# GpSimd splits each unit of weights in four pieces of 128x256 in place of one instruction over 128x1024

## The reference, cut to what matters

```python
def first_block(x, ...):
    u = rmsnorm(h, norm_mix[i])
    proj = u @ w_in[i]                      # attention and gated delta net inputs
    attn_out = sliding_window_sink_attention(aq, ak, av, sinks[i])
    dn_out = gated_deltanet(dq, dk, dv, dz, db, da, ...)
    h = h + jnp.concatenate([attn_out, dn_out], axis=-1) @ w_o[i]
    m = rmsnorm(h, norm_mlp[i])
    h = h + jnp.square(jax.nn.relu(m @ w_up[i])) @ w_down[i]
    gate = jax.nn.sigmoid(rmsnorm(h, norm_ple[i]) @ w_ple_gate[i])
    h = h + gate * (p[i] @ w_ple_proj[i])
    return rmsnorm(h, norm_final)

def second_block(x, ...):
    u = rms_norm(x, norm_mix_g[l]) @ w_in[l]
    y_pool, y_hgrn = pool_mixer(...), hgrn2_mixer(...)      # gated recurrence, 6 heads of 128
    x = x + jnp.concatenate([y_pool, y_hgrn], axis=-1) @ w_out[l]
    x = x + jnp.square(jax.nn.relu(rms_norm(x, norm_mlp_g[l]) @ w_up[l])) @ w_down[l]
    return rms_norm(x, final_norm_g)
```

## Time and profile before

| what | us |
|---|---|
| median of 3 runs | 2521.81 (2514.71 to 2522.38) |
| the profiled execution, device time | 2521.18 |
| its span in the profile | 2519.4 |
| PE busy | 2390.0 |
| DVE busy | 1881.2 |
| POOL busy | 1071.2 |
| ACT busy | 943.3 |

### The profile page before, as it was taken

How to read it: one execution, slowest core, us unless ns; L and a number is a source line. 1 busy time by engine, 2 the same in 40 slices (tenths; PEclk the granted TensorE clock), 3 DMA queues, 4 the chain that set the end, 5 groups by cost and what they waited for, 6 DMA issues and landing times. The chain is left out here.

```text
span 2519.4 us, 38470 instructions
## 1 busy us (share of the span) xinstructions
PE 2390.0 (95%) x15284; PEld 1899.3 (75%) x15284; DVE 1881.2 (75%) x2356; ACT 943.3 (37%) x1488; POOL 1071.2 (43%) x675
## 2 busy tenths in 40 slices
PE   8887999899999999999999999999999999999997
PEld 6655777687788877888777778777777888778885
DVE  3676666646878889888947677777568877988887
ACT  3154223214433334443514244444253333443433
POOL 3411222233555555454544433343445555555542
PEclk9998999999999999999999999999999999999998
DMA  4200000211244375434112111111314344644332
GB/s 162 68 17 17 27 27 27 80 48 42 103 173 147 138 246 182 157 126 167 42 65 95 53 34 35 35 35 43 117 34 147 138 146 162 244 167 151 131 123 99
DMA packets 109709, 254.99 MB, mean 101 GB/s; under 512 B 9312, under 2 KB 9568, under 8 KB 107360
## 3 DMA queue, kind: packets, MB, share of 16 engines
q1 hardware_dynamic: 104112, 233.82, 27.3%
q10 hardware_dynamic: 5424, 18.75, 2.2%
HBM read 182.28 MB, written 67.63 MB: 99 GB/s over the span
## 5 line engine op out<-in xcount | busy, mean ns | idle before, releaser
L681 PE MATMUL pairs<-x_hi,w_hi 128*128 128x512 f32 x1592 | 545.2, 407 | 36.5 <-DVE x_lo L1755 16.4
L681 PE MATMUL pairs<-x_lo,w_hi 128*128 128x512 f32 x1592 | 530.6, 397 | 0.8 <-issue 0.8
L681 PE MATMUL pairs<-x_hi,w_lo 128*128 128x512 f32 x1592 | 527.7, 396 | 0.8 <-issue 0.8
L681 PEld LDWEIGHTS pairs<-x_hi,w_hi 128*128 128x128 f32 x1592 | 286.9, 190 | 118.8 <-issue 37.8
L645 POOL TENSOR_TENSOR idle<-idle 128x1 f32<-128x1 f32 x78 | 19.5, 250 | 781.7 <-PE pairs L681 772.2
L681 PEld LDWEIGHTS pairs<-x_hi,w_lo 128*128 128x128 f32 x1592 | 299.4, 190 | 64.4 <-issue 0.9
L681 PEld LDWEIGHTS pairs<-x_lo,w_hi 128*128 128x128 f32 x1592 | 298.3, 190 | 62.9 <-issue 1.3
L664 POOL TENSOR_TENSOR w_lo<-w_raw,w_hi 128x512 fp32r<-128x512 f32 x150 | 238.1, 1596 | 230.1 <-ACT w_hi L1278 230.0
L681 PE MATMUL pairs<-work_r,w_hi 128*128 128x512 f32 x1072 | 329.9, 391 | 4.8 <-DVE work_r L1751 2.1
L681 PE MATMUL mid<-work_r,w_hi 128*128 128x512 f32 x992 | 309.6, 393 | 17.8 <-DVE work_r L1751 12.1
L664 POOL TENSOR_TENSOR w_lo<-work,w_hi 128x512 fp32r<-128x512 f32 x128 | 178.0, 1392 | 216.7 <-ACT w_hi L1278 216.7
(11 more groups left out here) (217 smaller groups left out, 3920.9 us busy)
## 6 DMA issues: line engine op xcount, KB each, us to landing
h_ops<-work SPq DMA_DIRECT2D x224, 256.0 KB, 4.4
w_raw<-w_stream SPq DMA_DIRECT2D x81, 512.0 KB, 3.5
w_raw<-w_up SPq DMA_DIRECT2D x120, 256.0 KB, 3.8
out_sq<-h_ops SPq DMA_DIRECT2D x28, 1024.0 KB, 5.2
x_lo_raw<-h_ops SPq DMA_DIRECT2D x28, 1024.0 KB, 5.1
work<-w_down SPq DMA_DIRECT2D x16, 1024.0 KB, 6.8
out_sq<-w_down SPq DMA_DIRECT2D x8, 1024.0 KB, 7.3
x_lo_raw<-w_down SPq DMA_DIRECT2D x8, 1024.0 KB, 5.5
```

Of the source, the lines that this page charges most:

```text
L681: return nc.tensor.matmul(out, w, x, start=start, stop=stop)
```

## The change

`split` issues the copy as four instructions over 256 columns each and the subtraction as four more. The waits and the signals stay: `w_hi_done` is raised by the last piece of the copy, `w_split` by the last piece of the subtraction.

```diff
+            PIECES = [slice(n * QUARTER, (n + 1) * QUARTER) for n in range(4)]
+
             def split(slot, loaded, started, n):
                 pool.wait_ge(w_loaded[slot], loaded)
                 if started is not None:
                     pool.wait_ge(unit_started, started)
                 nc.gpsimd.tensor_tensor(idle[:, 0:1], idle[:, 1:2], idle[:, 1:2], ALU.add)
-                nc.gpsimd.tensor_scalar(w_hi[:, slot, :], w_raw[:, slot, :], 1.0, None, ALU.mult).then_inc(w_hi_done, 1)
+
+                for part in PIECES:
+                    ins = nc.gpsimd.tensor_scalar(w_hi[:, slot, part], w_raw[:, slot, part], 1.0, None, ALU.mult)
+                ins.then_inc(w_hi_done, 1)
                 pool.wait_ge(w_hi_done, n + 1)
-                nc.gpsimd.tensor_tensor(w_lo[:, slot, :], w_raw[:, slot, :], w_hi[:, slot, :],
-                                        ALU.subtract).then_inc(w_split, 1)
+                for part in PIECES:
+                    ins = nc.gpsimd.tensor_tensor(w_lo[:, slot, part], w_raw[:, slot, part], w_hi[:, slot, part], ALU.subtract)
+                ins.then_inc(w_split, 1)
```

## The result

| | before | after |
|---|---|---|
| median | 2519.72 (2514.71 to 2522.38, 4 runs) | 2489.32 (2485.93 to 2493.17, 4 runs) |
| the profiled execution: device time, span | 2521.18, 2519.4 | 2492.07, 2490.3 |
| PE busy, and PE not busy in the span | 2390.0, 129.4 | 2387.1, 103.2 |

The ratio is 0.9875 [0.9862, 0.9888]: 30 us faster. The forecast was 11 faster, and its range ended at 2502, 13 above the result. Lines of the file moved by 6: the copy is L650, the subtraction L654, `idle` L647.

A forecast was written before the change was run, and what follows sets the result against it. PE, busy 2390.0 of 2519.4 us, was taken as the bound, with gains only where it waits for DVE. Gains of 14.3 less losses of 3.4 net 10.9 off 2521.2, so a median of 2511; range 2502 to 2525.

The forecast's parts named there:

- Pieces on POOL, holds on DVE: Unit splits: pieces of 0.73 (subtraction) and about 0.83 us (copy), a split 1.1 longer alone; lone DVE victims gain 1.6, crowds nothing.
- rival 3: POOL keeps its turn: DVE might be held through all four pieces, victims losing 0.5 more each; 2525 us, chance 0.08.
- Attention: PE's waits for DVE at 189.04, 125.92 and 161.81 get shorter by 2.4, 1.4 and 1.9 us.
- Seven taps, loss of 0.6: Convolution taps in a crowd on DVE at 216 to 227, ahead of PE's longest wait, lose 0.6 us.
- Delta net, 4.2 + 1.0 + 1.0: Three waits of 1.57 us gain 4.2, the wait at 340.03 and its twin at 421.5 gain 1.0, that at 486.58 1.0.
- The clock, a rival at 0.10: Between 116 and 515, shorter PE waits spare half the time at 1.2 GHz: another 5 to 9 us, 2503; chance 0.1.
- HGRN, 2.0 less 0.8 for unit 71: Crowd tails gain 0.7 us at one wait and 0.4 at each of three, 2 in all; unit 71's longer split loses 0.8.
- Gate and output product, 0.4: PE's waits there stand in rows of `x_lo`, crowds again: a gain of 0 to 0.4 us.
- Losses of ten crowds, 2: Ten other DVE crowds lose 0.2 us each, since four pieces are longer than one: 2 us.
- MLPs, nothing: The MLPs, half of the span, hold no split, so no gain or loss was counted there.
- Rival 1: What PE gains at one wait it loses at the next; if two thirds go, 2517 us; chance 0.27.
- Rival 2: The split becomes the bound: longer splits outlast their cover, lateness eating the gain at about +5.5 us; 2528 to 2549, chance 0.12.

The follow-up runs named there:

- 1.35 more of additions: Changed kernel (both parts in four) with six 128x1 additions ahead of the copy and three ahead of the subtraction, 0.9 and 1.35 us later: 2525.1 us, 1.0013.
- The memsets: Against the kernel before, copy and subtraction of the 78 units replaced by memsets to zero, so the split is left out: 2478.05 us, 0.9836.

## Why the prediction was wrong, step by step

The holds and the waits that they cause were read rightly, but the sum gave 10.9 of the 29.1 us. The largest part that it lacked is the clock's, 8.1 us, put at nothing; the rest are mostly waits that it sized too low.

- **Pieces on POOL, holds on DVE: right.** 0.84 and 0.72 a piece, the low end of both bounds; DVE gets its turn between pieces (rival 3 is out), and the place of 185.79 went as described.
- **Attention: right.** PE gained 2.37 where 2.4 was forecast, 1.80 for 1.4, 1.40 for 1.9.
- **Seven taps, loss of 0.6: wrong.** 2.3 gained. The step left out that the copy's short holds also free the fast one-input instruction that stood behind the subtraction.
- **Delta net, 4.2 + 1.0 + 1.0: right in mechanism, too small.** The three waits of 1.57 gave 5.4, those of 340 and 421.5 gave 1.2, the one of 486.58 gave 1.7: 8.3 for 6.2.
- **The clock, a rival at 0.10: the step that failed.** It was in no term of the sum, yet 8.1 us of busy time went between 116 and 515, 4.7 of them in the one window of the earlier trace rows. The rows for it were there; it stood apart as something that might happen, while each term that took a wait away implied it. The rival's 5 to 9 more held the number.
- **HGRN, 2.0 less 0.8 for unit 71: too small.** The three waits of 5.3 together went from 1.72, 1.71 and 1.86 to 0.31, 0.31 and 0.00, so 1.4 to 1.9 each where 0.4 was forecast. The step looked at the tails of crowds and missed single holds in them: ahead of the wait of 1.72 at 1580.31 a 128x256 instruction took 1.26 beside the whole copy, and takes 0.42 beside pieces. Unit 71 came late by 1.19, cost 1.4, and the wait behind it (the third, of 1.86) took that up, as forecast.
- **Gate and output product, 0.4: too small.** 3.1.
- **Losses of ten crowds, 2: not there** in the stages' times, though no run prices them alone. A piece of the copy costs DVE 0.2, and DVE was busy for 39 us less in all.
- **MLPs, nothing:** +3.3 and +1.6, with no instruction changed there. Of this 2.7 and 2.1 are busy time of the same matmuls, which is why PE's total fell by 2.9 only. "PE's busy time nearly the same" came true by this luck: 8.1 less in one stretch, 4.9 more in the MLPs. Kernels with the MLPs unchanged show from -2.5 to +8.0 in the first one. What sets it no run tells; it stays open.

The forecast of 10.9, plus 8.1 (clock), 5.2 (other idle time of PE between 116 and 515: 16.5 for 11.3), 4.2 (HGRN), 2.7 (gate, output product), 2.0 (crowds) and 0.7 (last head), less 4.9 (MLPs), is 28.9; the profile has 29.1.

Rival 1, given back, is out: PE stays ahead by what it wins. Rival 2 has the right mechanism, which these four pieces hardly meet (1.8 us of waits), and a wrong point. It set the added length at which lateness eats the gain at about +5.5 us, and counted 1.1. In HGRN the pieces already add 4.1, and 1.35 more of additions put the kernel 5 over before, though with 13.6 us of late splits only. The version with both parts in eight won 25 between 116 and 515 and ended at the time of before, with 18.7 us of PE's waits for late splits: the slower side was nearer than its 0.12 said.

One thing was assumed in all terms and not tested by the forecast: that the phase of before was a fair sample. Between 116 and 515 it was the worst of four, and that of after near the best for pieces: the size of the gain is in part luck of phase. Whole instructions ranged over 19 us in this stretch alone, and moving POOL by half a microsecond changed the whole program by 20 us with whole instructions and by 15, the other way, with pieces.

By the Trainium skill, "SBUF — State Buffer", section "Who interferes with whom", the one that comes first has the shared pair for the whole instruction. For the two-input subtraction the runs agree (tap of 3.50 beside a whole one of 2.37). For the one-input copy they agree only in part. A two-input DVE instruction was let in after 1.04 of 2.78, and takes 1.42 beside cut copies where 1.22 is its length alone. A fast one-input instruction of DVE ran at once when it came 1.32 or 1.49 us into a whole copy (182.25 above; 293.90 in the earlier trace rows), but one that came at 1.76 was held to the copy's end, in before and with the copy whole and only the subtraction cut (the rows below: the copy ends at 179.82, DVE's instruction of 0.17 at 179.84). So whether the small instruction is held was a matter of less than 0.5 us of phase. The same section of the Trainium skill says that an instruction with two inputs contends with a GpSimd instruction that reads, and not with one that only writes. The memsets agree: beside them no two-input instruction of 128x1024 is longer by over 0.2, and DVE is busy for 1777 us in place of 1881.

```profile
177.05 2.77 POOL L649 TENSOR_SCALAR w_hi<-w_raw 128x1024 fp32r<-128x1024 f32 x1
...
178.81 1.03 DVE L1844 TENSOR_SCALAR stat<-stat 128x4 f32<-128x4 f32 x1
```

## What to carry to other kernels

When two engines hold each other up, the instruction size of the one that has time to spare is worth a try, the two-input ones first: here the subtraction in four pieces and the copy whole gave 32 us and, with the MLPs, 42 to 45, while cutting both in eight gave nothing. But each of these was run at one phase, and the kernel with both parts in four lost its 30 us when it started 0.9 us later. So run a result of this kind at two or three phases, and beside it the uncut kernel at the same ones (20 us came from a later start alone), before calling it an effect of size. Before adding pieces, measure how early the splits end where the other engine works in a crowd, with one turn of the other engine added for each piece; that margin (1.54 us here), and not the average wait of 10 us, is what late splits use up. And where a wait goes that stands ahead of a stretch at the lower clock, put the clock into the sum.

## What the chip showed that was not expected

- The clock fell after some waits and not after others of the same length: 2.27 us of idle time at 495.02 in before was followed by 10.2 us at the lower level, 2.25 us at 474.90 in after by none. In before another wait of 2.24 stood 8 us ahead of it, in after one of 0.49.
- Small instructions of POOL take a turn as large ones do: eleven 128x1 additions take 1.6 us alone and 5.80 beside a crowd of DVE.
- A piece costs by its columns and about 0.2 us more, for the copy as for the subtraction: the copy takes 2.77, 1.49, 0.85 and 0.53 us for 1024, 512, 256 and 128 columns, the subtraction 2.40, 1.30, 0.74 and 0.46.
- A whole copy of 2.77 us is not one hold. Two-input instructions of DVE wait for its first 1.04 us only; fast one-input ones that read and write SBUF ran at once when they came 1.05 to 1.49 us into it, and were held to its end when they came at 1.76 to 2.15.
